# State outputs fetched in eight transfers behind a third weight, and four orders around them

## The reference, cut to what matters

```python
p = z @ w_in[l]                       # 7 slices of 1024 columns: u, q, f, i, og, ga, gb
y_a = s5_mixer(p[..., :o1], ...)      # state-space layer on u
y_b = hgrn2_mixer(q, f, i, og, ...)   # gated linear attention, 8 heads
merged = (jax.nn.sigmoid(ga) * (y_a @ w_ssm_proj[l])
          + jax.nn.sigmoid(gb) * (y_b @ w_hgrn_proj[l]))
...
y = (jnp.einsum('blgp,ghp->blgh', s_re, c_re) - jnp.einsum('blgp,ghp->blgh', s_im, c_im) + d_skip * uf)
y = jax.nn.gelu(y.reshape(bsz, L, SSM_WIDTH)); return y * jax.nn.sigmoid(y @ w_glu)
...
scores = jnp.where(causal, jnp.einsum('bhtd,bhsd->bhts', qi, ki), 0.0)
o = jnp.einsum('bhts,bhsv->bhtv', scores, v) + jnp.einsum('bhtd,bhdv->bhtv', qi, state)
```

## Time and profile before

| | us |
|---|---|
| median of 3 runs | 1741.4 |
| lowest, highest | 1739.86, 1742.45 |
| the profiled execution, its own time | 1741.52 |
| its span | 1739.7 |
| TensorE busy | 1684.5 (97%) |
| VectorE busy | 1098.1 (63%) |
| ScalarE busy | 748.0 (43%) |
| GpSimd busy | 301.1 (17%) |

### The profile page before, as it was taken

The page is one execution under the profiler, slowest core; times in us unless marked ns, Lnnn a source line. Parts: engine busy times, 40 slices in busy tenths (PEclk is TensorE's granted clock), DMA queues, the critical chain, the costliest instruction groups (busy, mean ns, idle before and its releaser), DMA issues.

```text
span 1739.7 us, 32474 instructions
## 1 busy us (share of the span) xinstructions
PE 1684.5 (97%) x12801; PEld 1494.7 (86%) x12801; DVE 1098.1 (63%) x1761; ACT 748.0 (43%) x1115; POOL 301.1 (17%) x289
## 2 busy tenths in 40 slices
PE   5999999999999999899999999999999999999998
PEld 4776666888888888899999999999999999989986
DVE  6767586777674678856868663344753766655633
ACT  4479574555332342632323544356223643323323
POOL 2122395220000003441015221110102000000002
PEclk8999999999999999999999999999999999999999
DMA  9454633343333332363336752233543233232332
GB/s 314 122 141 102 182 110 93 102 115 103 98 96 97 93 97 78 89 168 121 121 101 171 213 135 93 93 119 88 159 124 87 74 96 97 85 97 85 96 96 74
DMA packets 321168, 201.19 MB, mean 116 GB/s; under 512 B 51280, under 2 KB 303815, under 8 KB 320919
## 3 DMA queue, kind: packets, MB, share of 16 engines
q1 hardware_dynamic: 300976, 160.79, 32.7%
q0 software_dynamic: 7952, 24.83, 4.7%
q10 hardware_dynamic: 12118, 13.88, 2.3%
HBM read 177.75 MB, written 17.24 MB: 112 GB/s over the span
## 4 chain that ended last, share of the span: by engine, by line
PE 79%; DVE 8%; ACT 5%; SPq 2%; issue 2%; DMA 2%; POOL 1%; ACTq 0%; DVEq 0%; POOLq 0%
PE ps L1486 65%; DVE wlo L2214 2%; SPq L865 2%; PE ps L1627 1%; PE ps L1799 1%; PE ps L1686 1%; PE ps L1809 1%; ACT whi L923 1%; PE ps L1825 1%; DMA stage<-in_w_in_dram 1%; PE ps L1603 1%; PE ps L2057 1%; PE ps L2151 1%; DMA xrow<-in_x_dram 1%; SPq L714 1%
## 5 line engine op out<-in xcount | busy, mean ns | idle before, releaser
L1486 PE MATMUL ps<-zhi,whi 128*128 128x258 f32 (+2 forms) x2072 | 638.4, 308 | 1.4 <-ACT ub L1219 0.7
L1486 PE MATMUL ps<-zlo,whi 128*128 128x258 f32 (+2 forms) x2072 | 633.7, 306 | 0.0
L1486 PE MATMUL ps<-zhi,wlo 128*128 128x258 f32 (+2 forms) x2072 | 632.3, 305 | 0.0
L1486 PEld LDWEIGHTS ps<-zhi,whi 128*128 128x128 f32 x2072 | 391.3, 189 | 27.2 <-issue 4.0
L2214 DVE TENSOR_TENSOR wlo<-stage,whi 128x1024 fp32r<-128x1024 f32 x256 | 326.2, 1276 | 133.3 <-ACT whi L923 121.1
L1486 PEld LDWEIGHTS ps<-zhi,wlo 128*128 128x128 f32 x2072 | 391.1, 189 | 18.1
L1486 PEld LDWEIGHTS ps<-zlo,whi 128*128 128x128 f32 x2072 | 390.5, 188 | 18.8 <-issue 0.5
L923 ACT ACTIVATE whi<-stage 128x1024 fp32r<-128x1024 f32 x256 | 269.4, 1054 | 298.5 <-PE ps L1486 242.0
L1486 PE MATMUL ps<-ghi,whi 128*128 128x512 f32 x340 | 134.7, 396 | 0.0
L1486 PE MATMUL ps<-glo,whi 128*128 128x512 f32 x340 | 134.2, 395 | 0.0
L1486 PE MATMUL ps<-ghi,wlo 128*128 128x512 f32 x340 | 134.0, 394 | 0.0
(11 more groups left out here) (449 smaller groups left out, 2809.1 us busy)
## 6 DMA issues: line engine op xcount, KB each, us to landing
stage<-in_w_up_dram SPq DMA_DIRECT2D x88, 512.0 KB, 3.8
stage<-in_w_in_dram SPq DMA_DIRECT2D x74, 512.0 KB, 4.1
stage<-in_w_down_dram SPq DMA_DIRECT2D x32, 512.0 KB, 4.0
ring<-in_w_ada_dram POOLq DMA_DIRECT2D x24, 512.0 KB, 4.3
adab<-in_w_ada_dram SPq DMA_DIRECT2D x16, 512.0 KB, 7.8
stage<-in_w_down_dram SPq DMA_DIRECT2D x16, 384.0 KB, 3.4
stage<-in_w_o_dram SPq DMA_DIRECT2D x8, 512.0 KB, 4.1
ring<-in_w_ada_dram SPq DMA_DIRECT2D x8, 512.0 KB, 4.3
```

The source lines that it names most:

```text
L1486: last = pe.matmul(out, w(a, k), x(k, t0, t1), start=(k == 0 and a is whi and x is x_hi), stop=(k == ks - 1 and a is wlo))
```

## The change

Six edits, all of them in the stage told above:

1. `y_rows` reads all eight blocks of one group of sixteen partitions in one DMA. There are 8 DMAs of 264 KB in the place of 64 of 33 KB; the pieces of 264 bytes are the same and as many.
2. SP issues them behind the third `og` load, and not behind the second; the fourth load comes behind all of them (before, 48 of the 64 stood ahead of the third load, 8 ahead of the fourth and 8 behind it). ACT's wait for them is counted anew.
3. `outputs(b)` runs the products of `S` first, then waits for `TT`, then runs the products of `U`.
4. DVE runs `skip(1)` one pair of scan steps sooner, and ACT's `k_shift(1)` is written behind the third value job.
5. In `i3` ACT evicts value job j ahead of `gate_exps(j)`.
6. DVE runs `own_scores(0)` behind `into_gates(3)`, and not behind `into_gates(6)`.

```diff
-            def y_rows(k):
+            def y_rows(k, n):
-                y_view = y_dram[k].rearrange("(j h) g c -> g h j c", h=SH)
+                y_view = y_dram[k:k + n].rearrange("k (j h) g c -> g h (k j) c", h=SH)
                 for g in range(KD):
-                    sp.dma_start(y5[SH * g:SH * g + SH, k, :].rearrange("p (j c) -> p j c", j=LC), y_view[g])\
+                    sp.dma_start(y5[SH * g:SH * g + SH, k:k + n, :].rearrange("p k (j c) -> p (k j) c", j=LC), y_view[g])\
                       .then_inc(yT_in, 16)
...
-            loads("og", 0, 2)
+            loads("og", 0, 3)
             sp.wait_ge(ys_out, 16 * KD)
-            for k in range(6):
-                y_rows(k)
-            loads("og", 2, 3)
-            y_rows(6)
-            loads("og", 3, 4)
-            y_rows(7)
-            loads("og", 4, 8)
+            y_rows(0, KD)
+            loads("og", 3, 8)
...
                     if (c, j) == (0, 0):
                         k_evac(1)
-                    elif (c, j) == (0, 3):
+                    value_job(c, j)
+                    if (c, j) == (0, 2):
                         k_shift(1)
-                    value_job(c, j)
...
                 ahead("i3", j)
+                value_job(3, j)
                 gate_exps(j)
-                value_job(3, j)
...
-                    act.wait_ge(yT_in, 16 * KD * KD)
+                    act.wait_ge(yT_in, 16 * KD)
...
             def outputs(b):
-                pe.wait_ge(tt_in[b % 2], 16 * LC * (b // 2 + 1))
                 pe.wait_ge(scan_done, SCAN_STEPS)
...
-                for q in range(BP):
-                    for g in range(2):
-                        for m in range(2):
-                            pe.matmul(rows_of(m, g, q), TT[b % 2][:, 2 * q + g, 64 * m:64 * m + 64],
-                                      U5[:, 8 * b + 2 * q + g, :], start=q == 0, stop=False, skip_group_check=True)
...
-                                mm = pe.matmul(rows_of(m, g, q), WC[b % 2][r, q, c, SH + 64 * m:SH + 64 * m + 64],
-                                               S5[r, BP * b + q, c, 0:NC5], start=False, stop=c == 1, skip_group_check=True)
+                                pe.matmul(rows_of(m, g, q), WC[b % 2][r, q, c, SH + 64 * m:SH + 64 * m + 64],
+                                          S5[r, BP * b + q, c, 0:NC5], start=q == 0 and c == 0, stop=False, skip_group_check=True)
+                pe.wait_ge(tt_in[b % 2], 16 * LC * (b // 2 + 1))
+                for q in range(BP):
+                    for g in range(2):
+                        for m in range(2):
+                            mm = pe.matmul(rows_of(m, g, q), TT[b % 2][:, 2 * q + g, 64 * m:64 * m + 64],
+                                           U5[:, 8 * b + 2 * q + g, :], start=False, stop=True, skip_group_check=True)
...
                     scan(52 + 2 * (TB2 * c + j), 54 + 2 * (TB2 * c + j))
-                    if (c, j) == (0, 2):
+                    if (c, j) == (0, 1):
                         skip(1)
...
                 into_gates(h)
                 if h == 0:
                     decays(0, 1)
-                if h == 6:
+                if h == 3:
                     own_scores(0)
```

## The result

The changed kernel takes 1747.25 us (median of 8 runs, 1746.64 to 1749.59), the kernel before 1741.18 beside it. The ratio is 1.0032, 95% interval 1.0023 to 1.0042: 5.6 us slower, clear of noise. The forecast was 1735.8, with a range up to 1745.5; the time lies above the range, and on the other side.

The account below looks back on a forecast made before the run. TensorE, busy 97%, was taken as the bound, so only its idle time and low clock could be won. Gains of 1.8 + 0.3 + 2.15 + 1.5 = 5.75 us gave 1735.8 us; 8-in-10 range 1734.3 to 1745.5.

Parts of the forecast that it names:

- Y: Time for the merged fetch, 2.16 MB in 264-byte pieces, to drain ahead of the fourth og weight; taken as 14.4 us.
- the backlog at 987 us: Earlier trace's small fetches queued behind a weight, draining at about 150 GB/s; the source of the 14.4 us.
- The chain from the fourth weight to PE: `head_scores(1)` starts at the later of 1015.91 and the fourth og weight's landing + 3.41 us.
- The row of the copies from sixteen partitions: Copies of `K` into `TT`, all read from the same sixteen partitions, ran at 97 GB/s; used for the slow drain.
- The high bound: Fetch drain of 22.3 us, if a fetch writing sixteen partitions holds all sixteen queues to itself.
- The rival on the other side: Merged transfers go one by one through a limit of sixteen partitions: 22.3 us drain, 1745.2 us; chance 0.25.
- Change 4: Sooner `skip(1)` lets the `Vt` eviction come 1.82 us sooner; PE's gap falls from 2.24 to 0.42; gain 1.8.
- Change 3: The 64 products of `S`, run first, cover PE's 0.34 us wait for `TT`; gain 0.3 us.
- The issuing: SP's 8 issues of the merged fetch, at 0.43 us each, take 3.4 us, hidden by the fetch's own transfer.
- Changes 5 and 6: Remove PE's 0.89 and 0.75 us gaps, but only bring PE sooner to the wait on the fourth weight.
- The clock: With 1.25 us of idle time left ahead of `head_scores(1)`, PE's clock stays high: 1.5 us more gain.
- another stretch at low clock: In the sixteen-partition rival, longer idle time may cost a second half-clock stretch of 1.5 us, giving 1746.7 us.

Follow-up runs that it names:

- contig: Changed kernel with each transfer still writing sixteen partitions but reading 16,896 contiguous bytes for each partition, values scrambled; 1742.0 us, one run.
- flat16: Changed kernel with the 264-byte pieces read from other addresses into the same sixteen partitions, values scrambled; 1747.4 us, one run.
- flat32: Changed kernel with scrambled values and each of the eight transfers writing 32 partitions x 4 slots; 1738.2 us, one run.
- flat128: Changed kernel with scrambled values and each of the eight transfers writing all 128 partitions x 1 slot; 1734.8 us, one run.
- behind4: Changed kernel with the eight merged transfers behind the fourth og weight, not the third; ratio 1.0003 to the kernel before.
- scores_only: The kernel before with changes 5 and 6 alone; ratio 1.0002 (0.9993 to 1.0012).
- skip_only: The kernel before with change 4 alone; ratio 0.9992 (0.9983 to 1.0002), 1740.4 against 1741.8 us.
- behind2b: Second run of the changed kernel with the merged transfers behind the second og weight, not the third; ratio 0.9974 to the kernel before, 1737.4 us.
- b2_only: The kernel before with the merged fetch behind the second og weight, without changes 3 to 6; ratio 1.0004 (0.9995 to 1.0013).
- orders_only: Changed kernel with the old fetch put back, so changes 3 to 6 alone; ratio 0.9994 to the kernel before, 1741.1 us.

## Why the prediction was wrong

- **The step that failed is Y.** This is the time in which the fetch drains ahead of the fourth weight. It was put at 14.4 us from the backlog at 987 us in the earlier trace rows; it measured 24.2. Put into the prediction's own sum, 24.2 has `head_scores(1)` start at 1002.76 + 24.2 = 1027.0, 7.7 us later than before; less the 2.1 us of changes 3 and 4 that is 1747.1 us, and 1747.25 were measured. The chain from the fourth weight to PE was right. That it decides against the change from 18.6 us on agrees with contig, where 17.7 us went with 2 us less than the kernel before, in one run of each.
- **Why that row misled.** It had these pieces and this destination, but many small transfers queued together, so that several groups of sixteen partitions could be written at once. The prediction said so as its counterargument, and then did not follow it. That this is why the backlog moved at 150 is argued and not shown: the row covers 1 us, and no run here queued small transfers like that for longer. The row of the copies from sixteen partitions, at 97 GB/s, had the property that the change made decisive, and it was nearer: flat16, flat32 and flat128 show 93, 156 and 225. But it was near in part by luck. In the kernel before, in 890 to 892 us, the queues were busy little more than half the time, so this row shows no limit:

```profile
DMA  4465755664755543445647565665555555655455
```

In the drain of the changed kernel they are at 9 in every slice. The high bound (22.3 us) was taken for an end and was too low by 1.9.
- **The rival on the other side** was the right mechanism, with a chance of 0.25. Its price, 1745.2 us, was 2 us short. The estimate from the Trainium skill, "SBUF — State Buffer", section "Door 1: The DMA port swizzle", 104 GB/s and 1743.7 us, pointed the same way; the traces show 91 in this place with pieces of 264 bytes, 118 in another (behind4), and 122 with contiguous sources. Where the page and the trace differ, the trace decides. The page's advice to make single transfers large, which the prediction puts into the same section, stands in the one behind it, on the setup cost.
- **Change 4**: the gap of 2.24 went to 0.56 where 0.42 was forecast. Alone it gave 1.4 us by its ratio, between 3.0 less and 0.3 more time than before, and 1.3 us of idle time in its trace; the forecast was 1.8. Nothing here speaks against this term.
- **Change 3**: the 0.34 us are gone, at 919.95 to 922.72 the rows of PE follow on one another. Right.
- **The issuing** of the fetch was put at 3.4 us and took 18.77. It stayed hidden, as the fourth weight was issued at 1010.6 and landed at 1021.7.
- **Changes 5 and 6**: both gaps gone, worth nothing alone (scores_only), as the prediction said. Not foreseen: part of the 0.89 us belongs to the fetch that stood behind the second weight.
- **The clock**: forecast to stay high. It fell; but with Y right, the sum with the clock low as before is what fits. The rule behind the forecast, that it falls by the sum of the gaps, doesn't hold: in skip_only it stayed at 1.00 over gaps of 0.89, 1.44 and 0.66 us within 11 us, more than in the kernel before, and in behind2b it fell behind gaps of 1.06 and 0.65. So this term of 1.5 us had nothing to stand on.
- **Range and chances**: the range ended at 1745.5 because "another stretch at low clock" and a drain beyond the high bound were both given too little.

## What to carry to other kernels

Before you merge transfers, ask which partitions one of them writes: eight of sixteen partitions one after the other move at 91 to 118 GB/s here, and whatever stands behind them on the queue waits for them; what stands just ahead landed 1 to 3 us later than with nothing behind it. Put such a drain where the issuing engine would stand in a wait anyway; here the same transfers one weight sooner turned 5.6 us lost into 4 us won. Before you compare a time in two traces, count both from a point ahead of the change. When one term carries the forecast, choose its row by the property that the change makes decisive, not by how much else looks alike.

## What the runs showed of the hardware

- Writes in pieces of 264 bytes, 1024 for each transfer: 93 GB/s on 16 partitions, 156 on 32, 225 on 128. On 16 partitions contiguous sources of 16.9 KB gave 122. The same eight merged transfers on 16 partitions gave 91 to 118 in different places and traces.
- SP was held in issuing: eight merged transfers took 18.77 us to issue, most of them over 2.8 us each, and 3.94 us in contig. A queue so filled blocks the engine that issues. Row of the changed kernel (least, median, most in ns):

```profile
L865 SPq DMA_DIRECT2D y<-y_scratch x8: 746/2861/3382, 991.8 to 1007.6; - x8
```

- A transfer slows one that was issued before it on the same queue: the second `og` weight took 10.1 to 10.8 us from issue to landing with no fetch behind it, 11.3 to 11.5 with small transfers and 12.0 to 13.3 with merged ones.
- TensorE's clock went to 0.50 just behind one gap of 2.6 us (b2_only), at the end of one of 3.3 (orders_only), some 4 us into 10.8 us of idle time (the changed kernel), and behind two gaps of 1.06 and 0.65 us (behind2b). It stayed at 1.00 over gaps of 0.89, 1.44 and 0.66 us (skip_only). Full clock was granted again some 3 to 7 us after work had resumed.
